# Moving 32x32 blocks of a feed-forward tile between partition bands: GpSimd transfers in place of ScalarE copies

## The reference, cut to what matters

```python
h = rms_norm(x, norm_ffn[l])
gate_up = jnp.einsum('btd,df->btf', h, w_ffn_in[l])
ff_gate, ff_up = jnp.split(gate_up, 2, axis=-1)
x = x + jnp.einsum('btf,fd->btd', jax.nn.silu(ff_gate) * ff_up, w_ffn_out[l])
```

## Time and profile before

| what | us |
|---|---|
| median of 3 runs (2562.3 to 2562.54) | 2562.52 |
| the profiled execution, its own time | 2565.37 |
| its span, first to last instruction | 2563.6 |
| PE busy | 2546.2 |
| DVE busy | 1871.1 |
| ACT busy | 1306.2 |
| POOL busy | 18.7 |

### The profile page before, as it was taken

The page is one execution under the profiler, slowest core; times in us unless marked ns, Lnnn a source line. Parts: engine busy times, 40 slices in busy tenths (PEclk is TensorE's granted clock), DMA queues, the critical chain, the costliest instruction groups (busy, mean ns, idle before and its releaser), DMA issues.

```text
span 2563.6 us, 33953 instructions
## 1 busy us (share of the span) xinstructions
PE 2546.2 (99%) x11732; PEld 2117.6 (83%) x11732; DVE 1871.1 (73%) x2440; ACT 1306.2 (51%) x1667; POOL 18.7 (1%) x28
## 2 busy tenths in 40 slices
PE   9999999999999999999999999999999999999998
PEld 7888888888888888888888788888888888888887
DVE  6787768666567777777776776885698777777786
ACT  6545456554455555555555545555644444444443
POOL 0000000000000000000000000000000000000000
PEclk9999999999999999999999999999999999999999
DMA  8876767676568877788777587774477776677665
GB/s 308 271 256 210 232 214 239 201 234 220 188 195 261 257 259 252 256 257 259 255 258 257 169 248 234 222 221 149 156 234 229 219 218 218 218 216 219 212 217 181
DMA packets 281444, 584.30 MB, mean 228 GB/s; under 512 B 17968, under 2 KB 28384, under 8 KB 280432
## 3 DMA queue, kind: packets, MB, share of 16 engines
q1 hardware_dynamic: 279376, 574.25, 70.5%
q0 software_dynamic: 1952, 8.49, 1.1%
HBM read 580.54 MB, written 2.13 MB: 227 GB/s over the span
## 4 chain that ended last, share of the span: by engine, by line
PE 94%; DMA 2%; DVE 2%; ACT 1%; issue 0%; SPq 0%; DVEq 0%; ACTq 0%
PE acc L1306 82%; PE W L1306 10%; DMA raw<-in_w_in 2%; DVE wlo L1806 1%; PE W L1530 0%; ACT whi L634 0%; PE W L1388 0%; PE acc L1661 0%; DVE arena L1871 0%; DVE hHL L1878 0%; PE W L1498 0%; DVE raw L1819 0%; PE acc L1388 0%; DVE crow L1953 0%; DVE arena L2641 0%
## 5 line engine op out<-in xcount | busy, mean ns | idle before, releaser
L1806 DVE TENSOR_TENSOR wlo<-raw,whi 128x1024 fp32r<-128x1024 f32 x888 | 1081.7, 1223 | 643.4 <-ACT whi L634 640.2
L634 ACT ACTIVATE whi<-raw 128x1024 fp32r<-128x1024 f32 x888 | 937.1, 1059 | 1069.4 <-PE acc L1306 800.1
L1306 PE MATMUL acc<-whi,hHL 128*128 128x512 f32 x4992 | 1246.2, 391 | 2.3 <-ACT whi L634 1.8
L1306 PEld LDWEIGHTS acc<-whi,hHL 128*128 128x128 f32 x4992 | 932.2, 188 | 196.3 <-issue 2.5
L1306 PE MATMUL acc<-wlo,hHL 128*128 128x512 f32 x2496 | 668.9, 389 | 0.0
L1306 PEld LDWEIGHTS acc<-wlo,hHL 128*128 128x128 f32 x2496 | 468.5, 188 | 98.3 <-DVE wlo L1806 0.4
L1819 DVE CUSTOM_DVE_ANT_0 raw<-raw,crow 128x1024 f32<-128x1024 f32 x192 | 233.8, 1218 | 3.0 <-DMA raw<-in_w_ada_t 2.8
L1306 PE MATMUL acc<-whi,yH 128*128 128x512 f32 x768 | 209.6, 395 | 2.8 <-issue 2.8
L1306 PE MATMUL acc<-whi,yL 128*128 128x512 f32 x768 | 206.3, 390 | 0.0
L1306 PE MATMUL acc<-wlo,yH 128*128 128x512 f32 x768 | 205.5, 389 | 0.0
L1306 PEld LDWEIGHTS acc<-whi,yH 128*128 128x128 f32 x768 | 143.8, 188 | 33.3 <-issue 3.9
(11 more groups left out here) (222 smaller groups left out, 1115.7 us busy)
## 6 DMA issues: line engine op xcount, KB each, us to landing
raw<-in_w_in SPq DMA_DIRECT2D x264, 512.0 KB, 4.7
raw<-in_w_ada_t SPq DMA_DIRECT2D x192, 512.0 KB, 4.8
raw<-in_w_ffn_in SPq DMA_DIRECT2D x176, 512.0 KB, 4.6
raw<-in_w_up SPq DMA_DIRECT2D x128, 512.0 KB, 4.2
raw<-in_w_down SPq DMA_DIRECT2D x128, 512.0 KB, 4.5
raw<-in_w_ffn_out SPq DMA_DIRECT2D x88, 512.0 KB, 4.8
raw<-in_w_out SPq DMA_DIRECT2D x32, 512.0 KB, 4.3
raw<-in_w_o SPq DMA_DIRECT2D x32, 512.0 KB, 4.2
```

What stands on the lines that cost most here:

```text
L634: act.activation(whi[:, v], raw[:, s], ACT.Copy).then_inc(S("w_hi"), 1)
L1306: return pe.matmul(o, l, r, start=start, stop=stop, skip_group_check=True)
L1806: dve.tensor_tensor(wlo[:, v], raw[:, s], whi[:, v].bitcast(F32), ALU.subtract)\
```

## The change

In the loop over tiles 1 to 10, ACT no longer copies the 16 pieces. POOL waits for each tile's `ff_bank` and issues 16 transfers from `banked` to `gated_turned`, one per piece, each of 32 partitions x 1 KB; 10 waits and 160 transfers are written out in its program. A transfer adds 16 to `ff_moved` when it has landed, so ACT waits for 256 per tile. Tile 11 stays on ACT, with a semaphore of its own.

```diff
@@ gpsimd
             pool.dma_start(w2[:, 1], A["cmp_v_w2_2"]).then_inc(S("wg_in"), 16)
+            for n in range(10):
+                pool.wait_ge(S("ff_bank"), n + 1)
+                for b in range(16):
+                    pool.dma_start(bank(gated_turned, b % 4, b // 4), bank(banked, b // 4, b % 4)).then_inc(S("ff_moved"), 16)
             pool.wait_ge(S("h_mod_lo"), 8)
@@ scalar
                 for b in range(i, i + n):
                     ins = act.activation(bank(gated_turned, b % 4, b // 4), bank(banked, b // 4, b % 4), ACT.Copy)
-                if i + n == 16:
-                    ins.then_inc(S("ff_moved"), 1)
+                ins.then_inc(S("ff_shift"), 1)
             def ffn1(begin, down, n):
                 if down:
                     pl.phase("ffn1")
-                    for u in range(12):
+                    for _ in range(12):
                         hi()
-                        if u == 4:
-                            act.wait_ge(S("ff_bank"), n)
-                        if u >= 4:
-                            shift((u - 4) * 2, 2)
...
                 if down:
-                    act.wait_ge(S("ff_moved"), n)
+                    act.wait_ge(S("ff_moved"), n * 256)
...
             act.wait_ge(S("ff_bank"), 11)
             shift(0, 16)
-            act.wait_ge(S("ff_moved"), 11)
+            act.wait_ge(S("ff_shift"), 1)
             product_hi(slice(GT, 2 * GT))
```

## The result

| | before | after |
|---|---|---|
| median of 20 runs each, us | 2563.37 (2561.79 to 2565.85) | 2567.83 (2564.68 to 2571.7) |
| ratio, 95% interval | | 1.0017 (1.0011 to 1.0024) |
| profiled execution, own time, us | 2565.37 | 2568.35 |
| span, us | 2563.6 | 2566.6 |

The change costs 4.5 us (2567.83 - 2563.37), clear of the measurement's uncertainty, where no change was forecast; the time lies outside the stated range of 2560.8 to 2565.0. The runs also scatter more than before (7.0 us from lowest to highest, against 4.1).

A forecast was written before the change was run, and what follows sets the result against it. PE was taken to bound the kernel, busy 2546.2 of 2563.6 us. Every part of the change summed to 0: 2565.37 + 0 - 2.85 = 2562.5 us, range 2560.8 to 2565.0.

The forecast's parts named there:

- POOL's issues: On POOL, first network's feed-forward: 160 transfers at 0.54 us per issue, 8.6 us per tile, 86 us in all.
- The starved descriptors: POOL's issues beside DVE: the skill's 620 ns becoming 3100 would give near 2609 us; the prediction added nothing for it.
- Landing: POOL's transfers, issue to landing: 5.5 us taken, between 2.2 and 8.8; the first tile lands 7.3 us early.
- rival A: First tile lands late because each issue waits out a DVE instruction: 4.1 us stall, 2568.3 us with clock loss; chance 0.05.
- ACT's idle time before a split: ACT in the feed-forward: idle rises from 0.79 to about 1.6 us, still waiting for PE, worth 0 on the path.
- rival C: ACT's relief shows at the eleventh tile: at most 4.5 us faster, 2558.0 us; chance 0.02.
- Added to the DMA engines: Transfers beside weight loads: share 0.85 + 0.39 = 1.24 over 8.6 us, loads 2.1 us late at most, cost 0.
- the 6.9 us: Time to spare between the end of ACT's split after the first tile's copy into `yH` and PE's use of that unit.
- about the same margin: DVE's splits wait for ACT's and were said to have about as much to spare, 6.9 us.
- Rival B: Weight loads fall behind by packets: 8.5 us late, 1.6 over the margin, 3.3 us on ten tiles, 2595.5 us; chance 0.05.
- the 2 MB load: Nearest case in the trace, a POOL load of 272 packets: one weight split waited 4.50 us, PE stayed busy.
- 1.7 us of half clock: After the eleventh tile's copies and PE's 2.76 us idle: 3.45 us at clock 0.52, a loss the change leaves.

The follow-up runs named there:

- no moves: The changed kernel without the 160 transfers and without ACT's copies of tiles 1 to 10, so those blocks are not moved: 2564.89 us, ratio 1.0001 to the kernel before.
- slack probe: The kernel before, no transfers, with a needless 128x512 DVE addition in front of each down projection's second add: 2568.6 us, ratio 1.0017.
- add first: The changed kernel with DVE's second down-projection add in front of its product with `w_ada`, not behind it: 2566.44 us, ratio 1.0007 to the kernel before.
- before with add first: The kernel before, without transfers, with DVE's second down-projection add put in front of its product with `w_ada`: 2563.69 us, ratio 0.9997.
- copies and traffic: The kernel before, ACT's copies kept, with the same 160 transfers added into a spare place: 2568.59 us, ratio 1.0018.
- late moves: The changed kernel with POOL's transfers of tiles 2 to 10 waiting until the running down projection's fourth add is done: 2565.05 us, ratio 1.0001 to the kernel before.
- narrow traffic: The kernel before with ACT's copies and 160 added transfers into a spare place, rows of 256 bytes instead of 1 KB: 2565.67 us, ratio 1.0005.

## Why the prediction was wrong

**What held.** POOL's issues: 160 at 0.498 us (498/498/525 ns), 7.8 us per tile where 8.6 were reckoned, beside a DVE that is busy 72% of the stage. The starved descriptors of which the Trainium skill tells (page "SBUF — State Buffer", section "SBUF: two separate sides") did not show in these 160 issues, as the prediction had it. Landing: 5.1 us at the median (1.7 to 6.3), taken as 5.5. ACT's copy of the first tile into `yH` did not wait, so rival A falls:

```profile
783.62 1.04 ACT L1000 ACTIVATE yH<-arena 128x1024 fp32r<-128x1024 f32 x1
```

ACT's idle time before a split rose to 1.66 us, on PE, and its relief was worth nothing (no moves: 1.0001). The eleventh tile kept its cost (PE idle 2.79 us, then 3.46 us at clock 0.56), and rival C's bound of 4.5 us for it was right: sharing that tile gave 3.5.

**The step that failed** is the end of "Added to the DMA engines": loads fall behind by 2.1 us at most, and "they have the 6.9 us". The lateness was of the size that was reckoned (up to 1.3 us at DVE's product, 0.7 to 2.1 in the landings shown, 3.1 at most). That the size came near is in part luck: by the queue's share in that view a 1 KB row took 15.3% x 16 x 10.5 / 481 = 0.053 us of one DMA engine, half of what was taken as its bound, and with that, over the 7.8 us of issues, the prediction's sum gives 0.85 + 0.22 = 1.07, or 0.5 us. Why the loads were later than that is open. The margin is what was wrong. The 6.9 us belong to ACT's split and PE's use of it. A `w_ada` load is not split by ACT at all; DVE takes it in its order, with an add behind it that frees PE's accumulators, and the margin there is some 0.15 us by the trace before and 0.2 us by the slack probe. The sentence that DVE's splits have "about the same margin" speaks of the splits alone and leaves out what stands behind them. So a lateness well inside the stated margin stopped PE for 0.15 to 1.22 us on seven of the nine tiles whose transfers run beside a down projection, 4.4 us over the stage.

**Rival B** named the right mechanism with the wrong point: it decides at some 0.2 us of lateness, not at 6.9, and a tile then loses up to 1.22 us, not 3.3. Its price of 33 us came from packets; the narrow transfers speak for bytes. The comfort taken from the 2 MB load, beside which PE never stopped, did not carry over: it fell into a stage with no `w_ada` loads (SP's loads in that window are all of the projection weight).

## What to carry to other kernels

For added traffic, look for the margin on every engine that waits for a load, and follow that engine's order to whatever frees a buffer for the engine that bounds the kernel. The margin is the smallest of these, and it need not be on the split that feeds the matmuls. An engine at 100% without a wait says nothing of how close its releasers are. Here transfers in place of copies paid where the copies were on the path, and cost where their bytes met loads that something was waiting for; moving them by some 20 us was enough here to make them free.

## What was not expected of the hardware

Half a megabyte of SBUF-to-SBUF transfers within 8 us put back the weight loads beside it by 0.7 to 2.1 us in the tile shown, although the DMA engines' share of the stage rose only from 0.79 to 0.82.

The half clock behind the eleventh tile is not in every execution. Nine of the traces keep the sixteen copies there, and PE stops for 2.2 to 2.8 us in all nine. In six of them (before, after, no moves, add first, before with add first, slack probe) the clock then falls to the lower of its two levels, 1.2 GHz: 0.52 over 3.45 us before, 0.56 over 3.46 us after. In three (copies and traffic, late moves, narrow traffic) it stays at the upper one, 2.4 GHz. The windows of late moves, to be held against the earlier trace rows:

```profile
1412.46:1415.24 2.78, 0.00 (x0) 0.03 (x1) 2.78 (x4) 1.80 (x2) 0.00 (x0) 1.00 0.40 126
1415.24:1419.00 3.76, 3.76 (x17) 3.11 (x18) 3.30 (x3) 0.68 (x1) 0.00 (x0) 1.00 0.73 259
```

So the prediction's 1.7 us of half clock is a cost of some executions alone, and what decides between the two is open. In the two runs with the shared tile neither the stop nor the half clock is there. Their gains of 3.5 and 3.7 us lie between the stop alone, 2.8 us, and both, 4.5.
